# Weight slots at a 64-byte offset, two more chunks transposed through memory, and a new order for the last rows

## The reference

```python
h = rms_norm(x, norm_mix_pre[l])
proj = h @ w_in[l]
a_q, a_f, a_i, a_g, b_q, b_k, b_v, b_f, g_a, g_b = jnp.split(proj, split_points, axis=-1)
y_a = hgrn2_mixer(a_q, a_f, a_i, a_g, lb_table[l], hgrn_norm_w[l]) @ w_up_a[l]
y_b = fox_mixer(b_q, b_k, b_v, b_f + b_fox_f[l]) @ w_up_b[l]
merged = jax.nn.sigmoid(g_a) * y_a + jax.nn.sigmoid(g_b) * y_b
x = x + rms_norm(merged @ w_o[l], norm_mix_post[l])
h = rms_norm(x, norm_ffn_pre[l])
gate, up = jnp.split(h @ w_ffn_in[l], 2, axis=-1)
x = x + rms_norm((jax.nn.silu(gate) * up) @ w_ffn_down[l], norm_ffn_post[l])
```

## Time and profile before

| What | us |
|---|---|
| median of three executions | 2555.56 |
| the profiled execution | 2555.69 |
| its span, first to last instruction | 2553.9 |
| TensorE busy (granted clock 0.999) | 2544.0 |
| TensorE loading weights | 2121.1 |
| VectorE busy | 1513.2 |
| ScalarE busy | 1248.7 |
| GpSimd busy | 53.6 |
| DMA queue of the loads, share of 16 engines | 64.5% |
| of the chain that ended last: TensorE | 98% |

### The profile page before, as it was taken

How to read it: one execution, slowest core, us unless ns; L and a number is a source line. 1 busy time by engine, 2 the same in 40 slices (tenths; PEclk the granted TensorE clock), 3 DMA queues, 4 the chain that set the end, 5 groups by cost and what they waited for, 6 DMA issues and landing times.

```text
span 2553.9 us, 33053 instructions
## 1 busy us (share of the span) xinstructions
PE 2544.0 (100%) x13432; PEld 2121.1 (83%) x13432; DVE 1513.2 (59%) x1809; ACT 1248.7 (49%) x1582; POOL 53.6 (2%) x68
## 2 busy tenths in 40 slices
PE   9999999999999999999999999999999999999998
PEld 9878888888888888888888888888888888888887
DVE  6787776555455545576578554556655544555555
ACT  5576655444344434466455454534644444443443
POOL 0150000000000000000000000000000000000000
PEclk9999999999999999999999999999999999999999
DMA  8643557766676666776655566676577666776664
GB/s 302 179 163 120 173 172 248 222 215 211 193 226 209 212 191 214 216 228 216 190 174 165 166 175 194 186 262 197 197 217 227 209 195 209 216 221 195 208 206 149
DMA packets 172840, 515.03 MB, mean 202 GB/s; under 512 B 17104, under 2 KB 48080, under 8 KB 171632
## 3 DMA queue, kind: packets, MB, share of 16 engines
q1 hardware_dynamic: 172544, 512.77, 64.5%
q10 hardware_dynamic: 144, 0.15, 0.0%
HBM read 492.54 MB, written 19.92 MB: 201 GB/s over the span
## 4 chain that ended last, share of the span: by engine, by line
PE 98%; DVE 1%; ACT 1%; issue 0%; DVEq 0%; ACTq 0%
PE ps L516 97%; PE ps L520 1%; ACT W L1152 0%; DVE wlo L1711 0%; DVE W L1711 0%; ACT L1152 0%; ACT whi L1152 0%; DVE W L2381 0%; DVE h L1714 0%; DVE scr L1711 0%; DVEq L2696 0%; ACT scr L1152 0%; ACT sm L1152 0%; DVE RB L1787 0%; DVE W L2564 0%
## 5 line engine op out<-in xcount | busy, mean ns | idle before, releaser
L1711 DVE TENSOR_TENSOR wlo<-raw,whi 128x1024 fp32r<-128x1024 f32 x884 | 1080.3, 1225 | 946.1 <-ACT whi L1152 941.7
L1152 ACT ACTIVATE whi<-raw 128x1024 fp32r<-128x1024 f32 x884 | 933.8, 1059 | 1071.2 <-PE ps L516 1055.5
L516 PE MATMUL ps<-whi,xx 128*128 128x512 f32 x4160 | 1284.9, 390 | 0.0
L516 PEld LDWEIGHTS ps<-whi,xx 128*128 128x128 f32 x4160 | 777.7, 188 | 160.7 <-issue 0.7
L516 PE MATMUL ps<-wlo,xx 128*128 128x512 f32 x2080 | 809.6, 389 | 0.0
L516 PEld LDWEIGHTS ps<-wlo,xx 128*128 128x128 f32 x2080 | 390.4, 188 | 81.5
L516 PE MATMUL ps<-whi,hlo 128*128 128x512 f32 x944 | 368.6, 390 | 0.0
L516 PE MATMUL ps<-whi,hhi 128*128 128x512 f32 x944 | 367.4, 389 | 0.0
L516 PE MATMUL ps<-wlo,hhi 128*128 128x512 f32 x944 | 367.3, 389 | 0.0
L516 PE MATMUL ps<-xx,whi 128*128 128x512 f32 (+1 forms) x1088 | 310.8, 372 | 0.1
L516 PEld LDWEIGHTS ps<-xx,wlo 128*128 128x128 f32 x960 | 180.3, 188 | 37.9 <-DVE wlo L1711 1.2
(11 more groups left out here) (168 smaller groups left out, 916.5 us busy)
## 6 DMA issues: line engine op xcount, KB each, us to landing
raw<-in_gu SPq DMA_DIRECT2D x352, 512.0 KB, 4.3
raw<-in_w_in SPq DMA_DIRECT2D x256, 512.0 KB, 4.1
raw<-in_dn SPq DMA_DIRECT2D x176, 512.0 KB, 4.2
raw<-in_w_out SPq DMA_DIRECT2D x32, 512.0 KB, 3.7
raw<-in_w_up SPq DMA_DIRECT2D x32, 512.0 KB, 4.2
raw<-in_w_o SPq DMA_DIRECT2D x32, 512.0 KB, 4.3
W<-blocks SPq DMA_DIRECT2D x120, 128.0 KB, 2.7
blocks<-W SPq DMA_DIRECT2D x20, 512.0 KB, 6.3
```

The costliest lines, as they stand in the source:

```text
L516: return e.matmul(o, l, r, start=start, stop=stop, skip_group_check=skip)
L1152: return e.activation(o, i, f, **kw)
L1711: return e.tensor_tensor(o, a, b, op)
```

## The change

1. `whi` and `wlo` get slots of 1056 instead of 1024 elements, and items of kind `feat` and `half` stand 16 elements (64 bytes) into their slot. `tok` and `cmp` stay at the slot's start; slots are now 4224 bytes apart.
2. The last 1024 columns of the mixers' result go through memory as `o2` and `o3`, into two more `Hto`. They leave when SP is at units 546 and 551, VectorE transposes them in 2gb2. The eight last tiles are copied and subtracted from `Hto`. The 16 transposes of TensorE in 2gb3 are gone. The rows of w_up_b are reordered on the host. The reload of `h` from `keep` waits for the fox mixer's end instead of the transposes.
3. `forget` on ScalarE takes four units: Sigmoid, Sigmoid, two Ln, two Ln. VectorE's part begins one unit later.
4. `later(35)` in `gates` becomes `later(29)`.
5. The last rows of 2fd2_3: TensorE waits for the first rows' last matmul (`s_half`, 2), then does columns 0 to 255 of the four units and then columns 256 to 511, the latter into a bank of its own. VectorE adds in two steps, ScalarE squares in two steps, and the post of chunk 0 of the last rows is made by ScalarE (times `rs`) and GpSimd (sum), stored third.

```diff
-        whi = sb("whi", [P, NSPL, 1024], R)
-        wlo = sb("wlo", [P, NSPL, 1024], R)
+        whi = sb("whi", [P, NSPL, 1056], R)
+        wlo = sb("wlo", [P, NSPL, 1056], R)
...
-            return whi[:, q % NSPL, :], wlo[:, q % NSPL, :]
+            o = 16 if units[q]["item"]["kind"] in ("feat", "half") else 0
+            return whi[:, q % NSPL, o:o + 1024], wlo[:, q % NSPL, o:o + 1024]
...
-        for n in range(2):
-            chunks[f"o{n}"] = (len(chunks), end["2bf"] + 8 + 8 * n, (s_oa, 2), scr[:, :, n * 512:n * 512 + 512])
+        for n in range(4):
+            chunks[f"o{n}"] = (len(chunks), end["2bf"] + 8 + 8 * n if n < 2 else first["2gb2"] + (-1, 4)[n - 2], (s_oa, 2) if n < 2 else (s_fin, 8),
+                               scr[:, :, n * 512:n * 512 + 512])
...
+            def last_halves(it, u0):
+
+                on.wait_ge(s_half, 2)
+                for a in (0, 256):
+                    o = take("L")[:, 0:256] if a else pair_of(len(items) - 1)[1][:, 0:256]
+                    for u in range(u0, it["n"]):
+                        wh, wl = (w.rearrange("p (k n) -> p k n", n=CH) for w in slot(it["first"] + u))
+                        for kk, k in enumerate(it["ks"][u]):
+                            z = u == it["n"] - 1 and kk == 1
+                            mm(o, hlo[:, k, 128:256], wh[:, kk, a:a + 256], start=(a == 256 and u == u0 and kk == 0), stop=False, skip=True)
+                            mm(o, hhi[:, k, 128:256], wh[:, kk, a:a + 256], start=False, stop=False, skip=True)
+                            m = mm(o, hhi[:, k, 128:256], wl[:, kk, a:a + 256], start=False, stop=z, skip=True)
...
-            def o_tiles():
-                yield from later(4)
-                for k in range(8, 16, 2):
-                    tiles_T("x", XF["o"] + k, k * 128, scr, (s_fin, 8))
-                    yield
-
...
-                        square("G", tb, n, scr[:, tb, n * 512:n * 512 + 512])
+                        square("G", tb, n, scr[:, tb, n * 512:n * 512 + (256 if n == 3 and tb else 512)])
...
+                                act(junk[:, 256:512], scr[:, 1, 1792:2048], ACT.Square, accum_out=last).then_inc(s_sq, 1)
+                            on.wait_ge(s_gsum, tb + 1)
...
+                    if n == 3:
+                        on.wait_ge(s_rs, STAT["G"])
+                        act(scr[:, 1, 0:512], scr[:, 1, 0:512], scale=rs["G"][:, 1:2]).then_inc(s_gy, 1)
...
-                yield from later(35)
+                yield from later(29)
...
-                on.wait_ge(s_a, own.n)
+                read = own.n
+                yield
+                on.wait_ge(s_a, read)
                 act(ab[:, t:t + 4, :], ab[:, t:t + 4, :], ACT.Sigmoid).then_inc(s_sg, 1)
                 yield
                 on.wait_ge(s_lbd, 1)
                 on.wait_ge(s_sg, n + 1)
                 for q in range(t, t + 4):
+                    if q == t + 2:
+                        yield
...
                     tt(y, y, banks[tb], ADD).then_inc(s_sum, 1)
-                    on.wait_ge(s_sum, tb + 1)
-                    own.up(tt(G[:, tb, :], y, bcw[:, 1536:2048], MUL))
+                    on.wait_ge(s_sum, 1 + tb)
+                    a = 256 * tb
+                    if tb:
+                        own.up(tt(G[:, 1, 0:a], y[:, 0:a], bcw[:, 1536:1536 + a], MUL))
+                        on.wait_ge(s_sq, SQUARES["P"] + 8)
+                        g = gsum[:, 1:2]
+                        stt(g, parts["G"][:, 1, 3:4], 1.0 / D, g, MUL, ADD).then_inc(s_gsum, 1)
+                        on.wait_ge(s_unit, end[nm])
+                        tt(y[:, a:512], y[:, a:512], B("L")[:, 0:256], ADD).then_inc(s_sum, 1)
+                        on.wait_ge(s_sum, 3)
+                    own.up(tt(G[:, tb, a:512], y[:, a:512], bcw[:, 1536 + a:2048], MUL))
...
-                    for c in range(4):
+                    for c in range(tb, 4):
...
+            running.append(chain(blocks_o(2, 5), blocks_o(3, 5)))
+            walk(["2gb2"], side)
...
+            on.wait_ge(s_gy, 1)
+            o = h[:, 1, 0:512]
+            e.tensor_tensor(o, scr[:, 1, 0:512], o, ADD).then_inc(s_last, 1)
...
-                    on.wait_ge(s_tT, 14)
+                    on.wait_ge(s_fin, 8)
```

More of the change, by code:

```diff
@@ L275, in build @@
         Ht = W_(11264, 1024)
-        Hto = [W_(12288, 1024), W_(13312, 1024)]
+        Hto = [W_(12288 + 1024 * n, 1024) for n in range(4)]
         S0 = 8192
@@ L311, in build @@
         gsum = small(2)
+        glast = sm[:, 1279:1280]
         rsq = small(2, 128)
@@ L562, in unit @@
                             on.wait_ge(s_lo, q + 1)
-                            m = mm(o, xh_, wl[:, kk, :], start=False, stop=z)
+                            m = mm(o, xh_, wl[:, kk, :], start=False, stop=z or (it["name"] == "2fd2_3" and tb == kk == 1 and u == it["n"] - NSPL - 1))
                     elif it["kind"] == "half":
@@ L584, in first_unit @@
                 banks = pair_of(i)
-                wh = whi[:, 0, :].rearrange("p (k n) -> p k n", n=CH)
-                wl = wlo[:, 0, :].rearrange("p (k n) -> p k n", n=CH)
+                wh, wl = (w.rearrange("p (k n) -> p k n", n=CH) for w in slot(0))
                 on.wait_ge(s_hi, 1)
@@ L609, in units_by_block @@
                         for kk, k in enumerate(it["ks"][u]):
+                            if it["name"] == "2fd2_3" and tb:
+                                continue
                             if it["name"] == "2fg0" and tb == 0:
@@ L672, in walk @@
                                 units_by_block(i, it, last, it["n"])
+                                last_halves(it, last)
                         elif nm == "2o3" and u >= last:
@@ L1594, in o_tiles @@
                 for k in range(0, 16, 2):
[L1595 to L1602, removed]
+                    on.wait_ge(s_bt2, chunks["o1" if k < 8 else f"o{k // 4}"][0] + 1)
+                    on.wait_ge(s_unit, first["2gb3"] + k // 2 + 1)
+                    for kk in (k, k + 1):
+                        o, i = xhi[:, kk, :].rearrange("p (ta c) -> p ta c", c=32), by_tiles(Hto[kk // 4])[:, kk % 4]
+                        m = act(o, i, scale=C("hnw")[:, kk % 4:kk % 4 + 1]) if k < 8 else act(o, i)
+                        m.then_inc(s_xhi, 1)
                     yield
@@ L2593, in vector @@
             side = chain(side, fox())
-            walk([f"2g{x}{c}" for x in "ab" for c in range(4)][:7], side)
+            walk([f"2g{x}{c}" for x in "ab" for c in range(4)][:6], side)
+            running.append(chain(blocks_o(2, 5), blocks_o(3, 5)))
+            walk(["2gb2"], side)
             assert next(side, side) is side
@@ L2690, in sync @@
             for tb in range(2):
-                for c in range(4):
-                    on.wait_ge(s_post, 8 + 4 * tb + c + 1)
+                for c in ((0, 1, 2, 3), (1, 2, 0, 3))[tb]:
+                    on.wait_ge(*((s_last, 1) if tb and c == 0 else (s_post, 8 + 3 * tb + c + 1)))
                     e.dma_start(out[tb][:, c * 512:c * 512 + 512], h[:, tb, c * 512:c * 512 + 512]).then_inc(s_out, 16)
@@ L2851 @@
         "w_n2": narrow(bf),
-        "w_up": np.stack([pack(by_blocks(a["w_up_a_2"][0], range(2)), 4), pack(a["w_up_b_2"][0], 4)]),
+        "w_up": np.stack([pack(by_blocks(a["w_up_a_2"][0], range(2)), 4), pack(by_blocks(a["w_up_b_2"][0], range(2)), 4)]),
         "w_o": pack(by_blocks(a["w_o_2"][0], range(2)), 4),
```

38 lines of the change are left out of this document (24 added, 14 removed).

## The result

The changed kernel takes 2586.58 us (median of four executions, 2585.99 to 2587.3) where the kernel before takes 2555.52 beside it: 1.2% slower, a ratio of 1.0121 with a 95% interval of 1.0103 to 1.0139. The forecast was 2546.5 with a range to 2554.0; the time lies 31 us above the kernel before and 40 above the forecast. The span of the profiled execution is 2584.2 us, 30.3 more than before, at the same granted clock of 0.999 of the 2.4 GHz level.

What follows compares the result with a forecast made beforehand. TensorE, busy 2544.0 of 2553.9 us, was taken as the bound. From 2555.7, terms -6.6, -2.0, -0.7, -0.6 and +0.7 sum to -9.2, so 2546.5 us, range 2542.4 to 2554.0.

Steps and rivals of the forecast that it cites:

- Step 1: Stationary weights 64 bytes in, 1k, 1q0 and half items: 6.6 of 9.6 us excess goes; streamed weights keep their work.
- Rival (c): Shift makes half items' weight loads collide: +4.0 us there, 1k and 1q0 unchanged, 2557.1 us in all; chance 0.10.
- tok matmuls away from 227 ns: Sign against the forecast: streamed-weight matmuls of 512 columns leaving their old time of 226.7 ns each.
- rival (a): The stationary-weight excess goes wholly, -9.6 us in place of -6.6, giving 2543.5 us; chance 0.22.
- 69%: Share of the 9.6 us stationary-weight excess expected to go, taken from item 2bf at 115.4 ns a matmul: -6.6 us.
- (b): The shift gains nothing, by independent read ports or slipping phases: stationary-weight gain zero, 2553.1 us; chance 0.26.
- Step 2: Two more chunks through memory: four transposes in each of 2gb3's last four units go, -2.0 us.
- Step 3: Forget gates over four units: two TensorE stalls, placed in 2aq0- and 2aq0, both go, -0.7 us.
- Step 4: Softplus six units earlier: the 0.64 us TensorE stall at 249.65 goes, -0.6 us, ends -0.6 and +0.6.
- TensorE waiting near 225 us: Sign against the forecast: rows of TensorE waiting for wlo near 225 us.
- Step 5: Last rows in halves, in the tail: +0.7 us as GpSimd and VectorE exclude each other, ends -0.4 and +1.8.

Runs made afterwards that it cites:

- the kernel without item 1: Changed kernel with slots 1024 apart and no offset, all other parts kept: 2558.51 us, ratio 1.0011.
- the combined one: Changed kernel with slots 1152 apart, stationary weights 64, 192, 320 or 448 bytes in by slot, softplus and tail as before: 2549.11 us, ratio 0.9975.

## Why the prediction was wrong

Step by step, with its own numbers. What each part does is taken from the units' starts; the span is 30.3 us longer.

| step | predicted | measured |
|---|---|---|
| 1, weights as stationary | -6.6 | -2.2 in 1k and 1q0, -1.3 in the half units (1x2 and 2aq0 are counted under 4 and 3) |
| 1, weights as stream (`tok`) | 0, no term | +32.1 |
| 2, two chunks through memory | -2.0 | -2.0 |
| 3, forget gates | -0.7 | -0.9 |
| 4, softplus earlier | -0.6 | +4.5 by the rows, +4.8 by the run without it |
| 5, the last rows | +0.7 | +0.5 |
| until unit 1 starts, not of the change | 0 | -0.4 |

These add to +30.3, as the span.

**Step 1 failed, and alone decides.** Its sentence was that "streamed weights keep their work". They do, but not their place. I read the diff's 1056 as room for the offset and asked only what the offset does to the items that use it. The slot distance moves the other 760 units as well, by 0, 128, 256 and 384 bytes. The evidence that place matters at all was already in the argument: 119.8 ns against 113.3 for equal work, on which the whole item rests. Whoever believes that must ask the same of every operand that the edit moves, and `tok` has 9,120 matmuls against the 2,048 of `feat` and `half`. Rival (c) had the right kind of mechanism, a collision made by the new starts, and put it on the half items with +4.0 us as its end; on `tok`, 3.6 ns a matmul make 33. "Slower" had only 0.05 because the mechanism was bounded there. The last sentence of the prediction's list, "tok matmuls away from 227 ns", is what the chain shows.

The gain was mis-sized too: 3.7 us in place of 6.6. 1q0 takes 22.42 us against 23.48 and 1k 22.32 against 23.46, together 2.2 of the 2.5 us of excess: near rival (a), where all of it goes. A half group goes from 697 ns (2787 a unit) to 692 (2767 on average), not to 685: 1.5 of the 7.1 us. Taking 69% for both kinds from 2bf, whose loads are narrow, was the weak choice there.

The Trainium skill's rule, "SBUF — State Buffer", section "Who interferes with whom", gives TensorE two independent read ports and no waiting. By it the pad between `wlo` and `xx` changes nothing and gives 2555.5 us; the run gave 2606.3. The measurement decides: in this kernel the time of a matmul depends on where its two reads start against each other. The prediction used the rule as a rival to the gain (b). Its denial should have been weighed as a risk as well.

**Step 2 held.** 2gb3 takes 21.76 us without slow slots, in the kernel without item 1 and in the combined one, like its twin, against 23.61 before; the other 0.13 us are in the first unit of 2ua0. The waits of SP and the two transposes of VectorE cost nothing that the chain shows.

**Step 3 held,** with its place wrong: both stalls were in 2aq0, and both are gone; 2aq0- and 2aq0 are 1.0 us shorter together, 0.16 of it by step 1.

**Step 4 failed by its cover.** The old stall of 0.64 us is gone (1z0 is 0.7 shorter than with the softplus at its old place) and a new one of 3.99 stands in 1x2-. The cover that I named was the share of busy time over the whole span, 49% and 59%, and three units of split weights. In that stretch this cover did not help: the rows above show ScalarE held by two table loads between two copies, VectorE waiting for it and then with softplus's small operations, taps, splits and the products in one queue, and TensorE waiting for the products, not for `wlo`. The split weights ahead don't cover what VectorE makes besides. The prediction named "TensorE waiting near 225 us" as a sign against it, rightly, and had +0.6 as its end.

**Step 5 held in sum and in its parts.** In the changed kernel VectorE's tail is:

```profile
2570.50 0.69 DVE L1743 TENSOR_TENSOR scr<-scr,ps 128x512 f32<-128x512 f32 x1 [3.21 <-PE ps L520]
...
2576.56 0.42 DVE L1743 TENSOR_TENSOR scr<-scr,ps 128x256 f32<-128x256 f32 x1
...
2577.93 0.16 DVE L2039 RECIPROCAL sm<-sm 128x1 f32<-128x1 f32 x1 [0.50 <-ACT sm L1171]
...
2579.46 1.75 DVE L1746 SCALAR_TENSOR_TENSOR h<-W,sm,h 128x512 f32<-128x512 f32 x1
```

and GpSimd's beside it:

```profile
2578.93 1.73 POOL L2658 TENSOR_TENSOR h<-scr,h 128x512 f32<-128x512 f32 x1 [2370.72 <-ACT scr L1171]
```

The reciprocal ends 7.59 us after the first rows' addition began (predicted 7.70), the second addition of the last rows starts at 6.06 (6.27). GpSimd's addition takes 1.73 beside VectorE (1.1 estimated), and the post that meets it 1.75 instead of 0.75, the exclusion that the earlier trace rows showed in small; by the rule of the Trainium skill that the prediction cites for it, the trace agrees. The last post ends 10.71 after the zero, in the kernel before 10.19.

The range failed because its terms were bounded one by one while an operand with no term carried the result. A bound "from both sides" for the slots' distance, by the earlier trace rows alone (6.5 ns between the roles, times 9,120 `tok` matmuls), would have been 59 us in either direction.

## What to carry to other kernels

An edit to a buffer's size or order is an edit to the distance between every pair of operands behind it, and has to be costed on the matmuls that run most, not on those it is meant for. For float32r matmuls of 512 streamed weight columns, keep the start of the streamed operand and that of its stationary partner equal modulo 256 bytes, and check the time per matmul in the chain after any change of the memory map. Where operands have the other role, test the distance: there zero was among the slowest. Before a burst of table loads is moved, list what the queue of each engine holds in that stretch, not its share over the span.

## What the runs showed of the hardware that was not expected

- In `tok` units TensorE's rate depends on the distance between the starts of its two operands, modulo 256 bytes: 226.7, 228.9, 232.4 and 233.3 ns for 512 streamed columns at 0, 64, 128 and 192. Moving either operand alone by 128 bytes costs the same 16.5 us on 2892 matmuls, moving both costs nothing.
- The roles are not alike. With weights stationary and 256 columns of activations streamed, zero distance is the slowest: 120.0 ns, against 117.8, 118.6 and 117.8 with the weights 64, 128 and 192 bytes in. A clean half unit takes 2787, 2774, 2787 and 2760 ns at these distances, so there 128 bytes are as slow as zero. These are times with one distance in every slot; in the kernel before with slots 1056 apart, where zero and 128 take turns, half units take 2790 and 2815 and `feat` matmuls 120.0 and 118.3.
- The same addresses can have two rates. In the changed kernel `feat` units run at 113.3 ns from unit 2 until a few small matmuls come between at 45.5 us, and at about 117.8 in the last unit. Two units of 24 matmuls each, both in slot 3 (the table's x counts those that overlap the stretch):

```profile
37.36:40.08 2.72, 2.72 (x27) 1.00 0.72 214
48.79:51.62 2.83, 2.83 (x27) 1.00 0.50 114
```

  With slots 1152 apart and one offset, 64 or 192 bytes, they run at 117.8. With the same slots and offsets that change from unit to unit they run at 113.3, even where the offsets are 192 and 448 in turn, equal modulo 256. So for `feat` the distance modulo 256 alone does not fix the rate. What does was not tried further.
- A slow unit hands its rate on in the changed kernel: the first three matmuls of the next unit, which has a good distance, are still at 233 ns.
- A two-input addition of 128 x 512 float32 on GpSimd takes 1.73 us beside VectorE and stretches a VectorE operation of 0.75 to 1.75.
